# First stage of a gMLP, attention and MoE block on one core: x loaded first, and one half of the adaLN modulation summed on TensorE

## The chip, the cores and the metric

The kernel runs on one core of a Trainium2 chip. The metric is the device time of one execution in microseconds. It is written in Bass: each engine (TensorE, VectorE, ScalarE, GpSimd, and SyncE, which only issues transfers) has its own program, and semaphores order them.

## The reference

One layer on x (512 rows of 1024, f32), with a conditioning vector c. What matters here is its beginning:

```python
sc = silu(c)
mod = sc @ w_ada + b_ada                    # 1024 -> 6*1024
sh1, sc1, ga1, sh2, sc2, ga2 = split(mod, 6)
h = rmsnorm(x, g_pre_mix) * (1.0 + sc1) + sh1
proj = h @ w_in                             # 1024 -> 2560
...                                         # gMLP and attention branches, output projection
x = x + ga1 * rmsnorm(mixed @ w_out, g_post_mix)
h = rmsnorm(x, g_pre_ffn) * (1.0 + sc2) + sh2
...                                         # 64 experts, top 8, and a shared one
x = x + ga2 * rmsnorm(y, g_post_ffn)
```

## The kernel before

**Modulation.** w_ada is read in 24 pieces of 1 MB: six channels in the order SC1, SH1, GA1, SC2, SH2, GA2, four pieces each. A piece holds two of the eight k slices (128 partitions x 2 x 1024). VectorE weighs it (`weigh_piece`): for each slice, acc = slice * sc_col[k] + acc, in L1365 (the first slice) and L1367 (the others). acc then holds, for each partition, a partial sum; TensorE sums over the partitions. For the first two channels that is done in column form, eight matmuls of one moving column for each channel (L966), so that a1c and b1c (128x8) hold scale and shift by partition. For the four later channels `modulation_row` (L978) sums with a stationary tile of ones into rows.

**Loads.** SyncE issues c, pieces 0 and 1, the four tiles of x, and then the other pieces. Three slots hold the pieces (n modulo 3 up to n=8, then modulo 2), and a piece waits until VectorE has weighed the one that was in its slot (`ada_used`). w_in comes in ten pieces of 1 MB through GpSimd's queue into two buffers (L543); the first two wait until six pieces of w_ada have been weighed.

**h1.** ScalarE sums the squares of x (L691). VectorE, after its third piece, forms the rms factor (`factor`, L1342 to L1350), and ScalarE scales x into z1 (L697). TensorE waits for all four tiles of z1, transposes them in groups k=0 to 6 (`h1_transposes`, L949; seven PSUM banks, the eighth holds the columns), runs the column matmuls, and transposes group 7 into bank 4 once that has been read. VectorE makes a1c and b1c (L1395 to L1398, `ab_ok`). ScalarE then applies them for each k (L712), and VectorE splits the result into a high and a low part (L1409, L1410).

**w_in.** Each piece is split as well: ScalarE makes the high part (`piece_high`, L704), VectorE and GpSimd half of the low part each (`piece_low` L1403; L548). ScalarE and VectorE take up piece 0 behind k=3 of the h1 loop. `project(i)` (L1000) needs both low parts, and `project(0)` the first four k; it runs 48 matmuls. From the third piece on, VectorE alternates between `piece_low`, the norm of v and two pieces of w_ada for each piece of w_in.

Everything behind the projections (attention, output projection, router, 64 experts) is unchanged.

Of the kernel before, what the change touches and what calls it, by code (L numbers as in the profile page):

```python
# [21 lines left out]
F32 = mybir.dt.float32  # L22
# [3 lines left out]
ALU = mybir.AluOpType  # L26
# [9 lines left out]
WO_RING = 3  # L36
DG = 512
# [24 lines left out]
def block_kernel(nc, x, c, w_ada, b_ada, g_pre_mix, w_in, ln_sgu_g, ln_sgu_b, w_spatial, b_spatial,  # L62
                 g_branch, w_out, g_post_mix, g_pre_ffn, w_router, router_bias, w_gate, w_up,
                 w_down, ws_gate, ws_up, ws_down, g_post_ffn, out):
    with ExitStack() as ctx:
# [6 lines left out]
        def at(name, shape, dt, off):  # L72
# [11 lines left out]
        ada = [at("ada0", [P, 2, D], F32, 0), at("ada1", [P, 2, D], F32, 8 * KB),  # L84
               at("ada2", [P, 2, D], F32, 136 * KB)]
# [139 lines left out]
        vec_in = sem("vec_in")  # L225
        row_in = sem("row_in")
        grow_in = sem("grow_in")
        ada_in = [sem(f"ada_in{s}") for s in range(3)]
# [121 lines left out]
        def ada_slot(n):  # L350

            slots = [m % 3 if m < 9 else m % 2 for m in range(n + 1)]
            same = [m for m in range(n + 1) if slots[m] == slots[n]]
            return slots[n], len(same), same[-2] if len(same) > 1 else None

        CHUNKS = [SC1, SH1, GA1, SC2, SH2, GA2]
# [48 lines left out]
        def _(sp):  # L405
            sp.dma_start(c_col[:, :], c.rearrange("(p k) -> p k", k=KD)).then_inc(c_in, 16)
            for n in range(4 * len(CHUNKS)):
                g, q = CHUNKS[n // 4], n % 4
# [3 lines left out]
                slot, _, before = ada_slot(n)  # L412
# [8 lines left out]
                sp.dma_start(ada[slot][:, :, :], ada_v[:, 2 * q:2 * q + 2, g * D:(g + 1) * D])\  # L421
                  .then_inc(ada_in[slot], 16)

# [77 lines left out]
        def _(gp):  # L501
# [32 lines left out]
            for i in range(PIECES + 1):  # L534
                if i < PIECES:
                    if i == 0:
                        gp.wait_ge(ada_used, 6)
                    if i >= 2:
                        gp.wait_ge(wphi_ok, i - 1)
                        gp.wait_ge(wplo_dve, i - 1)  # L540
                        gp.wait_ge(wplo_pool, i - 1)
# [114 lines left out]
        def _(ac):  # L656
# [19 lines left out]
            with nc.allow_non_contiguous_dma(reason="two short vectors by column"):  # L676
                load(gb[:, :], g_branch.rearrange("(k p) -> p k", p=P))
                load(bsp[:, :], b_spatial.rearrange("g i -> i g"))
# [20 lines left out]
            def piece_high(i):  # L699

                ac.wait_ge(win_in[i % 2], 16 * (i // 2 + 1))
                if i >= 2:
                    ac.wait_ge(proj_mm, 4 * (i - 1))
                A(wphi[:, i % 2], wraw[:, i % 2], ACT.Copy).then_inc(wphi_ok, 1)  # L704


            ac.wait_ge(ab_ok, 1)
            for k in range(KD):
# [5 lines left out]
                if k == KH - 1:  # L714
                    piece_high(0)
# [26 lines left out]
            ac.wait_ge(ada_used, 9)  # L742
# [202 lines left out]
        def _(pe):  # L945
# [13 lines left out]
            for k in range(KD - 1):  # L959
                h1_transposes(k)  # L960

            for ch in range(2):
                pe.wait_ge(acc_ok, ch + 1)
                cols = acc[:, ch, :].rearrange("p (q k) -> p k q", k=KD)
                for k in range(KD):
                    ins = mm(ps[:, 7 * BANK + ch * KD + k:7 * BANK + ch * KD + k + 1], cols[:, k, :],  # L966
                             ones[:, 0:1], start=True, stop=True)
                ins.then_inc(mod_mm, 1)
# [3 lines left out]
            def modulation_row(ch):  # L972

                pe.wait_ge(acc_ok, ch + 1)
# [47 lines left out]
            pe.wait_ge(vec_in, 16 * 6)  # L1022
# [301 lines left out]
        def _(v):  # L1324
# [29 lines left out]
            def weigh_piece(n):  # L1354

                ch, q = n // 4, n % 4
                if q == 0 and ch >= 2:
                    v.wait_ge(mod_mm, ch - 1)
                slot, count, _ = ada_slot(n)
                v.wait_ge(ada_in[slot], 16 * count)  # L1360
                for r in range(2):
                    k = 2 * q + r
                    src = ada[slot][:, r, :]
                    if k == 0:
                        ins = V.tensor_scalar(acc[:, ch % 2, :], src, sc_col[:, 0:1], None, ALU.mult)  # L1365
                    else:
                        ins = V.scalar_tensor_tensor(out=acc[:, ch % 2, :], in0=src, scalar=sc_col[:, k:k + 1],  # L1367
                                                     in1=acc[:, ch % 2, :], op0=ALU.mult, op1=ALU.add)
                    if r == 0:
                        then(ins)  # L1370
                    else:
                        ins.then_inc(ada_used, 1)
                        v.wait_ge(ada_used, n + 1)
# [421 lines left out]
```

## Time and profile before

| | |
|---|---|
| median of 3 executions | 1143.39 us (1142.51 to 1143.91) |
| profiled execution | 1143.01 us |
| its span | 1141.3 us |
| TensorE busy in the span | 1044.1 us (91%) |
| VectorE / ScalarE / GpSimd busy | 720.5 / 570.9 / 592.6 us |
| start of `project(0)` | 53.98 us |

The times in rows are microseconds from the start of the span. The 1.7 us between the span and the profiled execution's own time lie outside of the trace. PE is TensorE's matmul part, PEld its weight loads, DVE VectorE, ACT ScalarE, POOL GpSimd, SP SyncE; a name that ends in q is that engine's sequencer, where transfers are issued. L966 is line 966 of the kernel before. A matmul on f32 operands is recorded as two matmul instructions, one on fp32r operands as one.

### The profile page before, as it was taken

Reading aid. Unit: us, or ns where it says so; the run is one execution under the profiler, and the core shown is the slowest. Engines: PE = TensorE matmul, PEld = TensorE weight load, DVE = VectorE, ACT = ScalarE, POOL = GpSimd, SP = SyncE. Lnnn points to the kernel's source line nnn. Section 1 sums busy time; section 2 is a strip of 40 time slices with the busy share of each in tenths; the row PEclk is TensorE's granted clock in tenths of the full one; section 3 lists DMA queues with packets and bytes.
Section 4 is the critical chain, followed back from the end, with each engine's and each line's share of the span. In section 5 each row is a group of like instructions: output and inputs, shape, how many; then the busy total and the mean of one; then the engine's idle time right before and its main releaser. Section 6 shows DMA issues by size and latency. Waiting matters only on the chain.

```text
span 1141.3 us, 15074 instructions
## 1 busy us (share of the span) xinstructions
PE 1044.1 (91%) x4500; PEld 726.2 (64%) x4500; DVE 720.5 (63%) x1282; ACT 570.9 (50%) x605; POOL 592.6 (52%) x356
## 2 busy tenths in 40 slices
PE   0699897979798899999999999999999999999965
PEld 0587675547663677666766677666776677666522
DVE  4649785652755665777666666567676666586247
ACT  4334125652341466655655566655665666555401
POOL 0223222540221576667767776776767777667300
PEclk9699998889998999999999999999999999999988
DMA  9656851202152489999999999999999888899296
GB/s 322 246 178 243 293 203 47 74 28 84 74 221 82 159 323 370 351 369 378 353 377 366 369 351 346 351 375 388 328 364 350 345 327 338 344 352 351 87 389 273
DMA packets 68904, 318.67 MB, mean 279 GB/s; under 512 B 18640, under 2 KB 19152, under 8 KB 41360
## 3 DMA queue, kind: packets, MB, share of 16 engines
q1 hardware_dynamic: 42096, 267.41, 61.3%
q0 software_dynamic: 23104, 47.50, 11.3%
q10 hardware_dynamic: 3680, 3.46, 0.9%
q8 instruction: 13, 0.21, 0.1%
q14 instruction: 11, 0.09, 0.0%
HBM read 317.25 MB, written 39.85 MB: 313 GB/s over the span
## 4 chain that ended last, share of the span: by engine, by line
PE 73%; DVE 9%; DMA 8%; issue 4%; ACT 3%; POOL 2%; SPq 1%; ACTq 0%; DVEq 0%; POOLq 0%
PE ps L1234 18%; PE ps L1215 10%; PE ps L1217 9%; PE ps L1216 9%; PE ps L949 7%; PE ps L1000 7%; DMA yall<-y_rows 4%; DMA rawd<-in_w_down_dram 3%; PE ps L1150 2%; PE ps L1125 2%; DVE acc L1367 1%; PE ps L1082 1%; PE ps L1056 1%; DMA ada<-in_w_ada_dram 1%; PE ps L1170 1%
## 5 line engine op out<-in xcount | busy, mean ns | idle before, releaser
L585 POOL DMA_INDIRECT hg<-h_rows,idxg x70 | 212.1, 3030 | 140.0 <-DVE idxg L1675 139.7
L827 ACT ACTIVATE whi<-raw 128x2048 fp32r<-128x2048 f32 x136 | 260.6, 1917 | 21.2 <-issue 10.4
L1681 DVE TENSOR_TENSOR wlo<-raw,whi 128x1536 fp32r<-128x1536 f32 x134 | 257.5, 1947 | 12.1 <-ACT whi L827 11.8
L1234 PE MATMUL ps<-rawd,actt 128*128 128x512 f32 x544 | 244.8, 592 | 2.0 <-ACT actt L863 1.4
L1215 PE MATMUL ps<-whi,hthi 128*128 128x512 f32 x544 | 225.2, 414 | 1.9 <-POOL wlo L600 1.9
L1695 DVE TENSOR_TENSOR htlo<-ps,hthi 128x1024 fp32r<-128x1024 f32 x68 | 83.2, 1224 | 206.3 <-ACT hthi L859 206.3
L1217 PE MATMUL ps<-whi,htlo 128*128 128x512 f32 x544 | 213.0, 392 | 0.0
L1216 PE MATMUL ps<-wlo,hthi 128*128 128x512 f32 x544 | 212.8, 391 | 0.0
L600 POOL TENSOR_TENSOR wlo<-raw,whi 128x512 fp32r<-128x512 f32 x134 | 208.0, 1575 | 1.9 <-ACT whi L827 0.2
L869 ACT ACTIVATE ysb<-ps 128x1024 f32<-128x1024 f32 x68 | 69.7, 1024 | 210.8 <-PE ps L1234 210.8
L1234 PEld LDWEIGHTS ps<-rawd,actt 128*128 128x128 f32 x544 | 102.5, 189 | 106.1 <-issue 97.8
L593 POOL DMA_INDIRECT y_rows<-ysb,idxs x68 | 72.8, 1070 | 100.0 <-ACT ysb L869 55.4
L1217 PEld LDWEIGHTS ps<-whi,htlo 128*128 128x128 f32 x544 | 102.1, 188 | 23.4
L1215 PEld LDWEIGHTS ps<-whi,hthi 128*128 128x128 f32 x544 | 102.2, 188 | 19.4 <-issue 2.0
L1216 PEld LDWEIGHTS ps<-wlo,hthi 128*128 128x128 f32 x544 | 102.7, 189 | 17.2
L949 PEld LDWEIGHTS ps<-ident,hg 128*128 128x128 f32 x552 | 64.6, 140 | 34.9 <-issue 34.8
L949 PE MATMUL ps<-ident,hg 128*128 128x128 f32 x552 | 71.6, 273 | 0.0
L859 ACT ACTIVATE hthi<-ps 128x1024 fp32r<-128x1024 f32 x68 | 69.5, 1022 | 0.7 <-PE ps L949 0.7
L1367 DVE SCALAR_TENSOR_TENSOR acc<-ada,sc_col,acc 128x1024 f32<-128x1024 f32 x42 | 62.9, 1499 | 8.7 <-DMA ada<-in_w_ada_dram 7.4
L548 POOL TENSOR_TENSOR wplo<-wraw,wphi 128x1024 fp32r<-128x1024 f32 x10 | 30.2, 3017 | 65.7 <-ACT wphi L704 65.6
L1660 DVE TENSOR_SCALAR s_onehot<-iotab,posb 128x128 bf16<-128x128 bf16 x284 | 52.6, 249 | 0.0
L560 POOL TENSOR_TENSOR wolo<-woraw,wohi 128x512 fp32r<-128x512 f32 x16 | 36.0, 2266 | 31.3 <-ACT wohi L797 24.9
(248 smaller groups left out, 1321.1 us busy)
## 6 DMA issues: line engine op xcount, KB each, us to landing
raw<-in_w_gate_dram SPq DMA_DIRECT2D x68, 1024.0 KB, 7.6
raw<-in_w_up_dram SPq DMA_DIRECT2D x68, 1024.0 KB, 10.5
rawd<-in_w_down_dram SPq DMA_DIRECT2D x68, 1024.0 KB, 12.8
ada<-in_w_ada_dram SPq DMA_DIRECT2D x24, 1024.0 KB, 6.9
yall<-y_rows SPq DMA_DIRECT2D x8, 2048.0 KB, 24.2
wraw<-in_w_in_dram POOLq DMA_DIRECT2D x10, 1024.0 KB, 5.8
woraw<-in_w_out_dram SPq DMA_DIRECT2D x16, 256.0 KB, 2.7
xs<-in_x_dram SPq DMA_DIRECT2D x4, 512.0 KB, 10.7
```

Source lines behind the costliest of these rows:

```text
L585: gp.indirect_dma_start(out=hg[s][:, :, :].rearrange("p k q -> p (k q)"), out_offset=None, in_=h_rows, in_offset=bass.IndirectOffsetOnAxis ...
L600: gp.tensor_tensor(wlo[s][:, :, c0:c1], raw[:, s, :, c0:c1], whi[:, s, :, c0:c1].bitcast(F32), ALU.subtract).then_inc(lo_pool, 1)
L827: A(whi[:, s, :, cols], raw[:, s, :, cols], ACT.Copy).then_inc(hi_ok, 1)
L949: return pe.transpose(o, i, ident[:, :])
L1000: ins = mm(bank(m), st, mv, start=(h == 0 and k == 0 and n == 0), stop=(h == 1 and k == KH - 1 and n == 2))
L1215: mm(out_, hthi[s][:, k, :], hi, start=(k == 0), stop=False)
L1216: mm(out_, hthi[s][:, k, :], lo, start=False, stop=False)
L1217: ins = mm(out_, htlo[s][:, k, :], hi, start=False, stop=(k == KD - 1))
L1234: ins = mm(bank(4 + hf), actt[:, k, :], rawd[:, s, k, hf * 512:(hf + 1) * 512], start=(k == 0), stop=(k == KF - 1))
L1367: ins = V.scalar_tensor_tensor(out=acc[:, ch % 2, :], in0=src, scalar=sc_col[:, k:k + 1], in1=acc[:, ch % 2, :], op0=ALU.mult, op1=ALU.add)
L1681: V.tensor_tensor(wlo[s][:, :, c0:c1], raw[:, s, :, c0:c1], whi[:, s, :, c0:c1].bitcast(F32), ALU.subtract).then_inc(lo_dve, 1)
L1695: V.tensor_tensor(htlo[s][:, :, :], bank(0, 2).rearrange("p (k q) -> p k q", k=KD), hthi[s][:, :, :].bitcast(F32), ALU.subtract).then_inc( ...
```

## The change

- SyncE issues c, all of x, and then pieces 0 to 5, without a wait, into six slots. Channels SH1 and SC1 alternate: even pieces n < 8 are shift, odd ones scale. Piece 6 goes into slot 0 and waits for `sh_mm` 1, piece 7 into slot 1 and waits for the first scale piece to be weighed. Behind piece 7 SyncE issues the first two pieces of w_in. The sixteen later pieces use two slots.
- The shift half is summed on TensorE: `shift_row(n)` multiplies with the stationary operand sc_col[:, k] (128x1) and 512 moving columns of the piece, four matmuls for each piece, into one row of banks 5 and 6. ScalarE copies the row to `sh_row` (1x1024), and eight matmuls with one contraction row bring it into column form.
- VectorE weighs only the scale pieces (four of the first eight), and forms the rms factor after the first of them.
- TensorE transposes five groups of z1 first, then the shift pieces, the shift columns and the scale columns, then groups 5 and 6.
- ScalarE makes the high part of w_in piece 0 between the row's copy and `ab_ok`, ahead of the h1 loop.
- The two short loads by column (gb, bsp) are issued by GpSimd, with a semaphore of their own.

```diff
-        ada = [at("ada0", [P, 2, D], F32, 0), at("ada1", [P, 2, D], F32, 8 * KB),
-               at("ada2", [P, 2, D], F32, 136 * KB)]
+        ada = [at(f"ada{s}", [P, 2, D], F32, (0, 8, 136, 112, 120, 128)[s] * KB) for s in range(ADA_SLOTS)]
+        sh_row = at("sh_row", [1, D], F32, 188 * KB)
...
+        FIRST = 8
+        ADA_SLOT = [0, 1, 2, 3, 4, 5, 0, 1] + [n % 2 for n in range(FIRST, 24)]
+        def ada_piece(n):
+            return (n % 2, n // 2) if n < FIRST else (n // 4, n % 4)
+        CHUNKS = [SH1, SC1, GA1, SC2, SH2, GA2]
...
 # SyncE
+            for t in range(TT):
+                sp.dma_start(xs[:, t, :], x[t * P:(t + 1) * P, :]).then_inc(x_in[t], 16)
             for n in range(4 * len(CHUNKS)):
-                if n == 2:
-                    for t in range(TT):
-                        sp.dma_start(xs[:, t, :], x[t * P:(t + 1) * P, :]).then_inc(x_in[t], 16)
-                if before is not None:
-                    sp.wait_ge(ada_used, before + 1)
+                g, q = ada_piece(n)
+                if n == FIRST:
+                    load_win(0)
+                    load_win(1)
+                if n == 6 or n == 8:
+                    sp.wait_ge(sh_mm, 1 if n == 6 else 4)
+                elif n == 7:
+                    sp.wait_ge(ada_used, 1)
+                elif n > 8:
+                    sp.wait_ge(ada_used, n - 5)
...
 # GpSimd
+                gp.dma_start(gb[:, :], g_branch.rearrange("(k p) -> p k", p=P)).then_inc(col_in, 16)
+                gp.dma_start(bsp[:, :], b_spatial.rearrange("g i -> i g")).then_inc(col_in, 16)
-            for i in range(PIECES + 1):
+            for i in range(1, PIECES + 1):
...
 # ScalarE
+            ac.wait_ge(sh_mm, 4)
+            A(sh_row[:, :], bank(5, 2)[0:1, :], ACT.Copy).then_inc(sh_ok, 1)
+            piece_high(0)
             ac.wait_ge(ab_ok, 1)
...
-                if k == KH - 1:
-                    piece_high(0)
...
 # TensorE
+            def shift_row(n):
+                _, q = ada_piece(n)
+                pe.wait_ge(ada_in[ADA_SLOT[n]], 16 * ada_count(n))
+                for r in range(2):
+                    k = 2 * q + r
+                    for hf in range(2):
+                        ins = mm(bank(5 + hf)[0:1, :], sc_col[:, k:k + 1], ada[ADA_SLOT[n]][:, r, hf * 512:(hf + 1) * 512],
+                                 start=(k == 0), stop=(k == KD - 1))
+                ins.then_inc(sh_mm, 1)
-            for k in range(KD - 1):
+            for k in range(5):
                 h1_transposes(k)
+            pe.wait_ge(sc_ok, 1)
+            for n in range(0, FIRST, 2):
+                shift_row(n)
+            pe.wait_ge(sh_ok, 1)
+            shifts = sh_row[:, :].rearrange("p (q k) -> p k q", k=KD)
+            for k in range(KD):
+                ins = mm(ps[:, 7 * BANK + KD + k:7 * BANK + KD + k + 1], shifts[:, k, :], ones[0:1, 0:1],
+                         start=True, stop=True)
+            ins.then_inc(mod_mm, 1)
+            pe.wait_ge(acc_ok, 1)
...
+            for k in range(5, KD - 1):
+                h1_transposes(k)
...
 # VectorE
-            for n in range(8):
+            for n in range(1, FIRST, 2):
                 weigh_piece(n)
-                if n == 2:
+                if n == 1:
                     factor(ST_X, D)
                     v.sem_inc(rs_x_ok, 1)
-            v.wait_ge(vec_in, 16 * 6)
+            v.wait_ge(vec_in, 16 * 4)
+            v.wait_ge(col_in, 16 * 2)
```

## Rows read from the trace of the kernel before

**Rows 1.** Busy time by stretch: start:end, length, busy (x instructions), clock, DMA.

```profile
350.00:1085.00 735.00, 727.16 (x3217) 502.48 (x3215) 470.88 (x931) 427.73 (x415) 495.30 (x278) 1.00 0.86 329
```

**Rows 2.** The chain of waits, first 120 us: start, length, what.

```profile
4.20 0.67 SPq L411
4.91 13.77 DMA ada<-in_w_ada_dram
18.77 1.29 DVE acc L1367
...
22.92 7.61 ACT z L697 x4
30.67 5.77 PE ps L949 x28
36.44 7.51 PE ps L966 x32
44.65 0.79 ACT h1f L712
...
53.98 24.75 PE ps L1000 x96
...
117.35 12.81 PE ps L1000 x48
```

**Rows 3.** DMA issues around 4.9, 25 and 4 us; last number: us to landing.

```profile
xs<-in_x_dram SPq DMA_DIRECT2D x1, 512.0 KB, 11.7
ada<-in_w_ada_dram SPq DMA_DIRECT2D x1, 1024.0 KB, 13.8
...
ada<-in_w_ada_dram SPq DMA_DIRECT2D x1, 1024.0 KB, 5.0
...
bsp<-in_b_spatial_dram ACTq DMA_DIRECT2D x1, 2.0 KB, 20.6
```

**Rows 4.** Timeline of VectorE and GpSimd, 10 to 60 us: start, length, instruction.

```profile
12.10 0.75 DVE L1365 TENSOR_SCALAR acc<-ada,sc_col 128x1024 f32<-128x1024 f32 x1 [12.10 <-ACT sc_col L680]
21.41 0.17 DVE L1342 TENSOR_SCALAR var<-stat 128x4 f32<-128x4 f32 x1
49.18 0.69 DVE L1410 TENSOR_TENSOR h1lo<-h1f,h1hi 128x512 fp32r<-128x512 f32 x1
50.45 1.23 DVE L1403 TENSOR_TENSOR wplo<-wraw,wphi 128x1024 fp32r<-128x1024 f32 x1 [0.58 <-ACT wphi L704]
50.50 3.37 POOL L548 TENSOR_TENSOR wplo<-wraw,wphi 128x1024 fp32r<-128x1024 f32 x1 [17.97 <-ACT wphi L704]
51.59 2.57 DVE L1409 CAST h1hi<-h1f 128x512 fp32r<-128x512 f32 x1
```

**Rows 5.** The chain of waits later on, 130 to 285 us.

```profile
130.16 1.72 PE ps L978 x4
...
158.89 0.87 PE ps L949 x8
...
197.84 4.56 PE ps L1056 x8
...
205.07 3.03 PE ps L1082 x8
...
238.75 0.98 PE ps L1090 x8
...
284.52 1.13 ACT o_sb L838
```

**Rows 6.** Stretches as in group 1; last three: granted clock, DMA share, GB/s.

```profile
30.00:40.00 10.00, 9.33 (x45) 9.37 (x45) 5.58 (x5) 0.52 (x1) 1.78 (x2) 0.96 1.01 378
...
59.00:60.00 1.00, 1.00 (x5) 0.76 (x4) 1.00 (x1) 0.00 (x0) 1.00 (x1) 0.63 0.31 115
...
118.00:119.00 1.00, 1.00 (x4) 0.78 (x3) 0.96 (x2) 0.00 (x0) 0.98 (x2) 0.50 0.07 29
...
206.00:208.00 2.00, 2.00 (x8) 0.83 (x6) 2.00 (x1) 1.50 (x3) 0.94 (x1) 0.87 0.00 0
```

More of the change, by code:

```diff
@@ L36 @@
 WO_RING = 3
+ADA_SLOTS = 6
 DG = 512
@@ L225, in block_kernel @@
         vec_in = sem("vec_in")
+        col_in = sem("col_in")
+        win_first = [sem(f"win_first{s}") for s in range(2)]
         row_in = sem("row_in")
         grow_in = sem("grow_in")
-        ada_in = [sem(f"ada_in{s}") for s in range(3)]
+        ada_in = [sem(f"ada_in{s}") for s in range(ADA_SLOTS)]
+        sh_mm = sem("sh_mm")
+        sh_ok = sem("sh_ok")
         ada_used = sem("ada_used")
@@ L349, in block_kernel, with ada_count @@
         SC1, SH1, GA1, SC2, SH2, GA2 = 1, 0, 2, 4, 3, 5
[L350 to L356, printed above, removed]
+        FIRST = 8
+        ADA_SLOT = [0, 1, 2, 3, 4, 5, 0, 1] + [n % 2 for n in range(FIRST, 24)]
+        def ada_piece(n):
+            return (n % 2, n // 2) if n < FIRST else (n // 4, n % 4)
+        def ada_count(n):
+            return ADA_SLOT[:n + 1].count(ADA_SLOT[n])
+        CHUNKS = [SH1, SC1, GA1, SC2, SH2, GA2]
         COLG = [DG, 0, 2 * DG, 2 * DG + 512, 2 * DG + 1024]
@@ L531, in _ @@
             gp.sem_inc(const_ok, 1)
-            for i in range(PIECES + 1):
[L535 to L541, printed above, removed]
+            with nc.allow_non_contiguous_dma(reason="two short vectors by column"):
+                gp.dma_start(gb[:, :], g_branch.rearrange("(k p) -> p k", p=P)).then_inc(col_in, 16)
+                gp.dma_start(bsp[:, :], b_spatial.rearrange("g i -> i g")).then_inc(col_in, 16)
+            for i in range(1, PIECES + 1):
+                if 2 <= i < PIECES:
+                    gp.wait_ge(wphi_ok, i - 1)
+                    gp.wait_ge(wplo_dve, i - 1)
+                    gp.wait_ge(wplo_pool, i - 1)
                     g, h = i // 2, i % 2
@@ L699, in piece_high @@
             def piece_high(i):
-                ac.wait_ge(win_in[i % 2], 16 * (i // 2 + 1))
+                if i < 2:
+                    ac.wait_ge(win_first[i], 16)
+                else:
+                    ac.wait_ge(win_in[i % 2], 16 * (i // 2))
                 if i >= 2:
@@ L1354, in weigh_piece @@
             def weigh_piece(n):
[L1356 to L1360, printed above, removed]
+                ch, q = ada_piece(n)
+                a = 0 if n < FIRST else ch % 2
+                if q == 0 and n >= FIRST:
+                    v.wait_ge(mod_mm, ch - 1 if ch > 2 else 2)
+                v.wait_ge(ada_in[ADA_SLOT[n]], 16 * ada_count(n))
                 for r in range(2):
                     k = 2 * q + r
-                    src = ada[slot][:, r, :]
+                    src = ada[ADA_SLOT[n]][:, r, :]
                     if k == 0:
-                        ins = V.tensor_scalar(acc[:, ch % 2, :], src, sc_col[:, 0:1], None, ALU.mult)
+                        ins = V.tensor_scalar(acc[:, a, :], src, sc_col[:, 0:1], None, ALU.mult)
                     else:
-                        ins = V.scalar_tensor_tensor(out=acc[:, ch % 2, :], in0=src, scalar=sc_col[:, k:k + 1],
-                                                     in1=acc[:, ch % 2, :], op0=ALU.mult, op1=ALU.add)
+                        ins = V.scalar_tensor_tensor(out=acc[:, a, :], in0=src, scalar=sc_col[:, k:k + 1],
+                                                     in1=acc[:, a, :], op0=ALU.mult, op1=ALU.add)
                     if r == 0:
```

32 lines of the change are left out of this document (14 added, 18 removed).

## The prediction

> **What bounds the kernel now.** I read the busy times by stage first [rows 1]: from 350 to 1085 us TensorE is busy 727 of 735 us, and nothing there is touched. The edit lies in front of the first projection. So the question is only when the first projection starts, and whether what follows moves with it.
>
> The chain of waits answers both [rows 2]. It runs from the third piece of w_ada, which lands at 18.7 us [rows 3], over VectorE (two products, then the rms factor), ScalarE's scaling of x (22.92 to 30.5), the 28 transposes (to 36.4), the two channels' column matmuls (to 43.95), a1c and b1c (44.6), half of the h1 loop, and `project(0)` at 53.98. Behind 53.98 every piece of the chain follows from the piece before it: TensorE to 78.7, ScalarE's evacuation and eight DMA issues, VectorE's weighing and layer norm, then TensorE again from 117.35. No wait there is for something that keeps its own time, so I let a shift of `project(0)` pass through at full size. The moved w_ada pieces need a check: with two slots piece n=10 is requested only when n=8 has been weighed, while before it had been in a slot since about 45 us. It is used a round of VectorE's loop later; a round goes with a projection piece, 24.75/2=12.4 us [rows 2], and a transfer with nothing ahead takes 5.0 [rows 3]. That is covered by 7 us.
>
> **The change, step by step (times of the profiled execution).**
> *x ahead, scale piece next.* Queue SP carried two pieces and x first; the last x landed at 4.20+11.7=15.9. The same 4 MB now go out as x, shift piece 0, scale piece 1, so piece 1 lands at 15.9. One MB more landed 2.8 us later (18.7) [rows 3]; pieces 2 to 5 land at 18.7, 21.5, 24.3, 27.1. ScalarE is free early (the long issue of bsp leaves its queue) and has its squares done by about 12; that is worth nothing, because VectorE's factor stands behind piece 1: 15.9+0.75+1.30=18.0, factor 1.5 (21.4 to 22.9 before), so z starts at 19.5 and ends at 27.1 (7.6 us for four) [rows 2, 4]. Here 3.4 us are won. The column loads on GpSimd's queue are needed at 50 us; the slower of the two took 20.6 us on the old queue [rows 3], and GpSimd has nothing else to do: zero.
>
> *What TensorE now does before piece 6 may be asked for.* SP's wait for n=6 is on `sh_mm`, the end of shift piece 0. TensorE comes to that only after `z_ok` and 20 transposes, 20x0.206=4.1 us: 31.2. Queue SP is then stuck with piece 7 and both w_in pieces behind it, and the DMA engines, busy all the time from 30 to 40 us before [rows 6], have nothing from 27.1 on.
>
> *Price of a shift piece.* It is 4 matmuls of 512 moving columns in f32. The nearest rows are the modulation rows: two such matmuls, recorded as four, took 1.72 us at the full clock, 0.43 a record [rows 5]. A piece is 8 records: 3.4 us at 2.4 GHz and 6.9 at 1.2. The stationary operand has one column where that row had 128; I take the same price, since a record's length in these rows goes with its moving columns (0.43 for 512, 0.12 for one). Bounds: above, the same; below, the one-column record, 0.12 (a piece 1.0 us, 1.9 at half).
>
> *Which clock.* The early rows run at 1.2 GHz though the granted clock reads 0.96 over 30 to 40: a transpose took 0.206 us then and 0.109 at 159 [rows 2, 5, 6]. The clock rose 5.6 us after `project(0)` began. In the attention stage it stayed low through 4.6 us of scores on 64 rows and rose about 1.2 us into the values' matmuls, whose stationary operand has 64 columns and 128 rows (they began at 205.07, the clock is up in 206 to 208) [rows 5, 6]. So a narrow stationary operand did not keep it low. I take a rise 3.5 us into piece 0 (bounds 1.2 and 5.6; never, as a rival). Half of 6.9 us is then done, the rest takes 1.7: piece 0 ends at 31.2+5.2=36.4.
>
> *Piece 6 onward.* Issued at 36.5, it lands after 5.0 us (a piece with nothing ahead of it [rows 3]): 41.5; piece 7 at 44.3, w_in 0 at 47.1, w_in 1 at 49.9. TensorE takes pieces 2, 4 and 6 without a gap: 36.4+3x3.44=46.7. ScalarE copies the row out of PSUM, 1.1 us as its 1024-column copy at 284 [rows 5]: 47.8. The eight shift columns are 16 records of 0.123 at the full clock, 2.0 us: 49.8. The scale half is ready (44.3+2.6=46.9), its columns take 2.0: 51.8. At 1.2 GHz these two would be 3.8 each (0.235 a record, as before).
>
> *A new collision.* ScalarE now makes wphi(0) ahead of the h1 loop: 47.8 to 49.7; GpSimd's wplo(0) runs 3.4 us, to 53.2. Before, a 512-column VectorE cast that came up while that instruction ran took 2.57 us and ended 0.3 after GpSimd (a subtraction of the same size, in another place, took 0.69); a1c's second operation, with two SBUF inputs, would meet it at 52.0. I count it held until 53.2: ab_ok at 53.6 instead of 52.4 [rows 4]. Nothing excludes a price of zero, so the low bound is 1.2 less.
> The Trainium skill (SBUF — State Buffer, "SBUF: two separate sides") says that VectorE and GpSimd share a port pair as an exclusive lock, which a VectorE operation with two SBUF inputs needs, and one with a PSUM input does not. By that rule a1c's first operation and b1c pass and only the second is held; the cast's row agrees that the loser waits to the end. With the rule the sum is as above, without it 1.2 us less.
>
> *The h1 loop.* Before, from ab_ok (44.6) four steps of VectorE went to 49.9, but wphi(0), placed at k=3, made wplo(0) end at 53.87, and that started `project(0)` [rows 4]. Now wplo(0) is done; only VectorE's own part of 1.23 stands behind the fourth step: 5.3+1.25, so `project(0)` starts 6.6 behind ab_ok where it was 9.4. 2.8 us are won. The two transpose groups behind the columns and the last group (bank 4) fit in these 6.6 us. wplo(1) still follows the h1 loop and so trails `project(0)` by what it did; the chain shows the two projections without a gap.
>
> *Sum.* 53.6+6.6=60.2, against 53.98: +6.2. In parts: z 3.4 us earlier; 8 transposes fewer ahead 1.6; shift rows 15.5; copy 1.1; columns 3.5 cheaper at the full clock; collision 1.2; h1 loop 2.8 cheaper: -3.4-1.6+15.5+1.1-3.5+1.2-2.8=+6.5, which agrees within the rounding of the handovers. The profiled execution took 1143.01 (span 1141.3), the median of the others is 1143.39, so I add to the median: 1149.6. I leave `project(0)`'s own slow 5.6 us as they are: the engine again has about 5 idle us ahead of it.
>
> **Rivals.**
> *The clock never rises on the shift rows* (1.2 GHz throughout). For it: one column of the array is far less than the 64 of the values' rows, and 5.8 us of transposes and 7.5 us of one-column matmuls did not raise it [rows 2]. Pieces 4x6.9=27.5: 31.2 to 58.7; copy 59.8; columns 7.6: 67.4; ab_ok 68.1; `project(0)` 74.7: +20.7, 1164.
> *The clock is still high when `project(0)` begins.* The old one lost 5.6/2=2.8 us there. For it: TensorE is now busy until 53 rather than 44. Against it: after the pause ahead of 117.35 the clock read 0.50 from 118 on, and here about 5 idle us lie ahead of `project(0)` [rows 2, 6]. +3.4: 1146.8.
> *Columns at 1.2 GHz.* The clock falls again while one-column matmuls run: 7.6 for 4.0, the collision gone: +8.7, 1152.1. This, and a piece 6 that lands 2.4 us later than I count (an estimate; 1.6 of it is hidden behind pieces 2 and 4), are the upper side of my own case.
> *Not slower: the one-column stationary operand is cheap.* At 0.235 us a record a piece is 1.9: piece 0 ends at 33.1, piece 6 lands at 38.1, piece 7 at 40.9, the row is out at 41.2, columns to 45.7 at the full clock, ab_ok 46.4 if nothing holds it, `project(0)` 53.0: -1.0, 1142.4. It decides only if a shift record costs under about 0.25 us and the collision is absent (GpSimd would run to 49.3). The moving rows of the modulation matmuls speak against it [rows 5].
> *The loss is swallowed later*, 1143.4: some wait behind 53.98 would need a clock of its own. The row loads and the w_ada pieces are the candidates, but all are requested by events that shift too, and the chain of before waits for none of them between 53.98 and 117.35.
>
> **How the numbers follow.** My case 0.64, with its upper side; clock still high 0.12; never rises 0.10; cheap operand 0.05; swallowed 0.04; something that I don't see 0.05. A measurement tells about 0.2% (2.3 us) from no change. My case, the high clock and the never-rising clock are all slower; with half of the unseen: 0.88. Cheap operand, swallowed: same 0.08 after giving a little to each side; faster 0.04. My own case's bounds: early rise and no collision take 2.3 off, to 1147.3; late rise (+1.1), slow piece 6 (+0.8) and slow columns (+2.5) add 4.4, to 1154.0. The range reaches down over the high clock with an early rise (1145.5) and up to 1156.5 for a rise later than the rows above show; the never-rising clock stays out.
>
> **What the profile of the changed kernel would show.** z from 19.5 to 27; SP's wait for n=6 ending on TensorE at about 36, with the DMA engines near empty from 27 to 38; shift records that come every 0.86 us and from within piece 0 on every 0.43; `project(0)` at about 60; first evacuation of v at about 85. Wrong if z starts near 13 (factor not held by piece 1), if piece 6 is issued before 31, if shift records stay at 0.86 or show 0.25, or if `project(0)` moves by 6 and the end does not.

## The result, and the profile after

| | before | after |
|---|---|---|
| median (6 runs each, taken side by side) | 1143.07 us (1141.3 to 1144.6) | 1148.37 us (1146.72 to 1149.18) |
| ratio, 95% interval | | 1.0047 [1.0029, 1.0065] |
| profiled span | 1141.3 us | 1147.5 us |
| start of `project(0)` | 53.98 us | 63.88 us |
| last vv row evacuated | 182.5 us | 190.7 us |
| last read of y_rows asked for | 1088.95 us | 1097.49 us |

The changed kernel is slower by 5.3 us in the median and by 6.2 us in the span. The forecast was 1149.6 us, and the sign, the time and the range hold. The way there holds less well: `project(0)` moved by 9.9 us where 6.2 were forecast, and 3.7 of those were given back before the end.

The chain of waits of the changed kernel, for the same stretch as [rows 2], with two rows of its end (start, length, what):

```profile
3.71 13.72 DMA ada<-in_w_ada_dram
17.53 0.76 DVE acc L1407
18.32 1.29 DVE acc L1409
21.15 7.49 ACT z L716 x4
28.77 4.50 PE ps L972 x20
33.27 14.51 PE ps L989 x32
47.80 1.02 ACT sh_row L730
48.87 3.96 PE ps L1001 x16
52.83 3.91 PE ps L1007 x16
57.47 0.79 ACT h1f L737
...
63.88 24.32 PE ps L1042 x96
...
1097.49 38.34 DMA yall<-y_rows
```

L989 is `shift_row`, L1001 the shift columns, L1007 the scale columns, L972 the transposes, L1042 `project`. The order is the one that the prediction drew: piece 1, factor, z, transposes, shift rows, copy, columns, h1 loop. VectorE has left it from 19.6 to 57 but for the factor and a1c; the 14.5 us of L989 stand where nothing stood before.

SyncE's waits in the changed kernel (engine and line, what it waited for: us, times, longest), and the stretches around the moved work, columns as in [rows 1]:

```profile
SPq L442 <- PE ps L989: 34.4, 2, 26.5
```

```profile
26.00:28.00 2.00, 0.00 (x0) 0.00 (x0) 0.32 (x1) 2.00 (x2) 0.00 (x0) 1.00 0.11 43
30.00:32.00 2.00, 2.00 (x12) 2.00 (x11) 0.29 (x1) 0.00 (x0) 0.00 (x0) 1.00 0.00 0
51.00:52.00 1.00, 1.00 (x6) 1.00 (x6) 0.00 (x0) 0.00 (x0) 1.00 (x1) 0.82 1.02 414
52.00:54.00 2.00, 2.00 (x10) 1.99 (x10) 0.00 (x0) 0.00 (x0) 1.04 (x1) 0.50 1.02 414
```

The moved matmuls and the columns of the changed kernel by line (duration ns min/median/max, first and last start, forms), the first row for 33.2 to 34.2 alone:

```profile
L989 PE MATMUL ps<-ada,sc_col x2: 881/946/1011, 33.2 to 34.0; 128*1 128x512 f32 x2
L989 PE MATMUL ps<-ada,sc_col x32: 592/592/1011, 33.2 to 47.2; 128*1 128x512 f32 x32
L1001 PEld LDWEIGHTS ps<-ones,sh_row x16: 307/330/331, 48.9 to 52.4; 1*128 1x128 f32 x16
L1001 PE MATMUL ps<-ones,sh_row x16: 371/371/392, 48.9 to 52.5; 1*128 1x1 f32 x16
L1007 PE MATMUL ps<-ones,acc x16: 376/376/397, 52.8 to 56.3; 128*128 128x1 f32 x16
```

The 32 records of L989 fill 14.51 us; from about 34.7 on they come every 0.43. The DMA engines, at 1.01 from 30 to 40 before [rows 6], carry nothing from about 27 to 38: queue SP stands at piece 6, which waits for the end of shift piece 0, and piece 7 and both w_in pieces stand behind it. That was forecast. It looks like the fault of this design; the experiments say that it is not.

### The profile page after: what moved, and what is told of

The parts are those of the page before. It is cut to its first block, busy times and chain, and to the rows that moved or that the text cites. A ratio compares the mean times of both kernels' runs of the same rounds, so it can differ in the third digit from the quotient of the medians.

```text
span 1147.5 us, 15128 instructions
## 1 busy us (share of the span) xinstructions
PE 1059.3 (92%) x4532; PEld 729.5 (64%) x4532; DVE 710.6 (62%) x1274; ACT 571.5 (50%) x606; POOL 588.2 (51%) x356
## 4 chain that ended last, share of the span: by engine, by line
PE 77%; DVE 9%; DMA 6%; issue 3%; ACT 2%; POOL 1%; SPq 1%; ACTq 0%; DVEq 0%; POOLq 0%
PE ps L1276 19%; PE ps L1257 11%; PE ps L1259 10%; PE ps L1258 10%; PE ps L972 7%; PE ps L1042 7%; DMA yall<-y_rows 3%; PE ps L1192 2%; PE ps L1167 2%; PE ps L1124 1%; DMA rawd<-in_w_down_dram 1%; DVE acc L1409 1%; PE ps L989 1%; PE ps L1098 1%; DMA ada<-in_w_ada_dram 1%
## 5 line engine op out<-in xcount | busy, mean ns | idle before, releaser
L607 POOL DMA_INDIRECT hg<-h_rows,idxg x70 | 186.2, 2660 | 141.7 <-DVE idxg L1718 139.4
L622 POOL TENSOR_TENSOR wlo<-raw,whi 128x512 fp32r<-128x512 f32 x134 | 230.3, 1741 | 2.1 <-ACT whi L850 0.3
L972 PEld LDWEIGHTS ps<-ident,hg 128*128 128x128 f32 x552 | 64.6, 141 | 35.0 <-issue 34.8
L972 PE MATMUL ps<-ident,hg 128*128 128x128 f32 x552 | 71.6, 273 | 0.0
L1409 DVE SCALAR_TENSOR_TENSOR acc<-ada,sc_col,acc 128x1024 f32<-128x1024 f32 x35 | 53.9, 1540 | 24.3 <-DMA ada<-in_w_ada_dram 23.4
## 6 DMA issues: line engine op xcount, KB each, us to landing
rawd<-in_w_down_dram SPq DMA_DIRECT2D x68, 1024.0 KB, 13.3
```

What stands on the lines that cost most here:

```text
L607: gp.indirect_dma_start(out=hg[s][:, :, :].rearrange("p k q -> p (k q)"), out_offset=None, in_=h_rows, in_offset=bass.IndirectOffsetOnAxis ...
L622: gp.tensor_tensor(wlo[s][:, :, c0:c1], raw[:, s, :, c0:c1], whi[:, s, :, c0:c1].bitcast(F32), ALU.subtract).then_inc(lo_pool, 1)
L972: return pe.transpose(o, i, ident[:, :])
```

## The experiments

All were timed in five rounds against the kernel before. The theory behind the prediction (T) says that the change loses because TensorE takes up the shift pieces only after z and the transposes, and needs longer for them than it took for what was removed. Its first rival says that the DMA pause sets the end.

**1. Eight slots, so that SyncE stops for nothing before piece 8.** From the changed kernel:

```diff
-(0, 8, 136, 112, 120, 128)[s] * KB) for s in range(ADA_SLOTS)]
+(0, 8, 136, 112, 120, 128, 176, 96)[s] * KB) for s in range(ADA_SLOTS)]
...
-                if n == 6 or n == 8:
-                    sp.wait_ge(sh_mm, 1 if n == 6 else 4)
-                elif n == 7:
+                if n == 8:
+                    sp.wait_ge(sh_mm, 1)
+                elif n == 9:
                     sp.wait_ge(ada_used, 1)
...
```

> Changed kernel, but eight slots: pieces 6 and 7 and both w_in pieces are issued without a wait. Theory 1 (the loss is TensorE's order: it takes up the four shift pieces one behind the other after the transposes, 33.3 to 47.8 us, and no piece is late for it): project(0) stays at 63.9, within 0.5, and the time is that of the changed kernel, 1148.4, though piece 7 is weighed at about 31 to 35 instead of 45.7 and the pause of the DMA engines from 26 to 38 us is gone. Theory 2 (the loss is SyncE's wait for n=6 and the pause behind it): project(0) comes 5 to 10 us earlier and the time falls to 1139 to 1144.

Measured: 1147.5 us, ratio 1.0035 [1.0022, 1.0047]; `project(0)` at 62.37. A stretch and the chain:

```profile
26.00:28.00 2.00, 0.00 (x0) 0.00 (x0) 0.55 (x1) 2.00 (x2) 0.00 (x0) 1.00 1.03 412
```

```profile
20.84 7.48 ACT z L716 x4
28.46 3.98 PE ps L972 x20
32.43 13.84 PE ps L989 x32
```

The pause is gone, DMA share 1.03 where it was 0.11, and VectorE took up its last scale piece at 32.6 instead of 45.75. The shift rows still start at 32.4 and `project(0)` is only 1.5 us earlier, where T had allowed 0.5 and the rival had asked for 5 to 10. The 1.5 us are no wait of SyncE's: z starts 0.3 earlier, the same 20 transposes take 3.98 us for 4.50, and the shift rows 13.84 for 14.51, as the matmuls reached the fast pace within the transposes and not within the rows. Such a difference comes without any edit too: the 28 transposes of the old kernel take 5.77 us in its own profile, 5.03 in that of experiment 8 and 4.63 in that of experiment 7. A difference of 1 us in `project(0)` between two profiles is therefore no evidence by itself. The pause was hidden behind TensorE's own queue: the rival falls.

**2. The shift pieces as they land.** From the changed kernel; TensorE takes pieces 0, 2 and 4 ahead of its wait for z, and piece 6 behind the transposes:

```diff
-            pe.wait_ge(z_ok, TT)
...
-            for k in range(5):
-                h1_transposes(k)
             pe.wait_ge(sc_ok, 1)
-            for n in range(0, FIRST, 2):
+            for n in range(0, FIRST - 2, 2):
                 shift_row(n)
+            pe.wait_ge(z_ok, TT)
+            for k in range(5):
+                h1_transposes(k)
+            shift_row(FIRST - 2)
```

> Changed kernel, but TensorE takes shift pieces 0, 2 and 4 as they land, ahead of its wait for z and the transposes; only piece 6 stays behind them. Theory 1 (order on TensorE): three pieces, 10 to 11 us, leave the path; transposes end at 33.3, piece 6 is done at 37 to 40, project(0) at 53 to 56, 8 to 10.5 us earlier than 63.9. The time is then 1138 to 1141 if the 4 us that the changed kernel showed less at the end than at project(0) belong to the change, 1142 to 1144 if they were chance of its last read and of ScalarE's issues. Theory 2 (the DMA pause): the same direction, as piece 6 is asked for at about 22, so only its agreement with the eight-slot run decides between the two.

Measured: 1135.05 us, 0.9927 [0.9910, 0.9945]. The chain:

```profile
5.45 19.50 DMA ada<-in_w_ada_dram
...
24.99 3.59 PE ps L988 x8
...
28.63 2.40 PE ps L972 x20
31.03 3.54 PE ps L988 x8
```

`project(0)` starts at 50.67, 13.2 us ahead of the changed kernel (8 to 10.5 were expected), and the time follows by 13.3. Two things add up: three pieces lie under the wait for z, and the matmuls have reached the fast pace before the transposes, 20 of which take 2.40 us (0.120 each) instead of 4.50. The same matmuls, slots, loads and columns, in another order, turn a loss of 5 us into a gain of 8. That is the largest effect of the study, and T's main point. Against the kernel before only 3.3 of the span's 8.4 us are won at `project(0)`; 2.2 more have come by the last vv row, and 2.3 by a faster last read (38.42 us for 40.70), on which see experiments 9 and 10.

**3. The factor ahead of the first scale piece.** From the changed kernel:

```diff
+            factor(ST_X, D)
+            v.sem_inc(rs_x_ok, 1)
             for n in range(1, FIRST, 2):
                 weigh_piece(n)
-                if n == 1:
-                    factor(ST_X, D)
-                    v.sem_inc(rs_x_ok, 1)
```

> Changed kernel, but VectorE forms the rms factor before piece 1, as soon as the squares of x are summed (12 us). z then runs from 13.5 to 21, the transposes to 25.5, the shift pieces 0, 2 and 4 follow as they have landed (the last at 25), and piece 6 is asked for at about 30. Theory 1 (order on TensorE, headed by z): project(0) 7 us earlier than 63.9, at 56 to 57.5, time 1140.5 to 1142. Rival: z is not what TensorE's chain hangs on (it waits for shift pieces or for piece 6 instead), project(0) at 60 or later, time 1145 and more.

Measured: 1141.05 us, 1.0001 [0.9989, 1.0013]; `project(0)` at 56.86. The chain:

```profile
14.59 7.45 ACT z L716 x4
22.17 4.50 PE ps L972 x20
26.67 14.09 PE ps L989 x32
```

z starts 6.6 us earlier, everything behind it moves by as much or a little more, and the loss is gone from the time. It is not gone from the first stage: `project(0)` is still 2.9 us later than in the kernel before, and the last read, 38.35 us for 40.70, gives most of that back. x had been there and squared since about 12; the factor, a chain of 0.17 us operations, stood behind 1 MB of w_ada.

**4. Both orders together.** Experiment 2 with the edit of experiment 3:

> Both: shift pieces 0, 2, 4 taken up as they land, and the factor before piece 1. With z ready at 21 TensorE's transposes come after piece 4 (landed at 25) instead of at 28.6, so piece 6, which lands at about 30, is the next bound. Theory: project(0) at 49.5 to 50.7, 0 to 1.2 us earlier than with the landing order alone, time 1134 to 1135. Rival: piece 6 lands as early as 28, then 2.4 us earlier, time 1132.5.

Measured: 1128.98 us, 0.9915 [0.9881, 0.9948], the lowest median of the kernels that compute the reference; its six executions spread from 1126.4 to 1137.8. The chain:

```profile
28.49 2.33 PE ps L972 x20
30.83 3.54 PE ps L988 x8
34.39 1.02 ACT sh_row L730
35.45 3.96 PE ps L1002 x16
39.41 3.91 PE ps L1008 x16
```

Here `project(0)` is at 50.47, 0.2 earlier than in experiment 2: there already the transposes followed piece 4's matmuls (24.99+3.59=28.58), so the earlier factor has nothing left to give. The time is 6 us lower all the same. The last vv row came at 173.1 (177.0 in experiment 2), and half of that difference is one place where VectorE weighs a piece; its timeline there, first of experiment 2 and then of this one:

```profile
82.08 9.40 DVE L1410 SCALAR_TENSOR_TENSOR acc<-ada,sc_col,acc 128x1024 f32<-128x1024 f32 x4
```

```profile
80.81 7.38 DVE L1410 SCALAR_TENSOR_TENSOR acc<-ada,sc_col,acc 128x1024 f32<-128x1024 f32 x4
```

The same four products take 9.40 and 7.38 us: two of them meet GpSimd's subtraction and last 3.3 us each in experiment 2, one does in this one, and the others take 1.3. The two kernels' intervals overlap, so a gain of this one over experiment 2 is not shown.

**5. Columns from a contiguous stationary operand.** A column matmul loads every eighth element of `acc` or `sh_row` as its stationary operand, since feature p*8+k belongs to column k. From the changed kernel, here it loads 128 neighbours:

```diff
-            shifts = sh_row[:, :].rearrange("p (q k) -> p k q", k=KD)
+            shifts = sh_row[:, :].rearrange("p (k q) -> p k q", k=KD)
-            cols = acc[:, 0, :].rearrange("p (q k) -> p k q", k=KD)
+            cols = acc[:, 0, :].rearrange("p (k q) -> p k q", k=KD)
```

> Changed kernel, but the 16 column matmuls read their stationary operand as 128 neighbouring elements instead of every eighth; the columns then hold the wrong features, so the output is not the reference's, and the time is read for the price alone. Theory A (the price of 0.247 us a record is that of a strided weight load, whatever the clock): 0.12 to 0.15 us a record at the full clock, the two groups take 4 to 5 us instead of 7.9, project(0) at 60 to 61, time 1145 or so. Theory B (the low clock): 0.24 us a record as before, project(0) at 63.9, time 1148.4.

The features get each other's scale and shift, which changes the routing (536 expert transposes instead of 552), so only the first stage is read; the time, 1125.72 us, can't be set beside the others. `project(0)` starts at 60.20, within the 60 to 61 of theory A. The rows of the two column lines, to set beside those of the changed kernel above:

```profile
L1001 PEld LDWEIGHTS ps<-ones,sh_row x16: 181/187/187, 48.0 to 49.7; 1*128 1x128 f32 x16
L1001 PE MATMUL ps<-ones,sh_row x16: 245/245/266, 48.0 to 49.7; 1*128 1x1 f32 x16
L1007 PEld LDWEIGHTS ps<-ones,acc x16: 186/333/333, 49.9 to 52.6; 128*128 128x128 f32 x16
```

The columns take 5.1 us instead of 7.9. In the changed kernel the granted clock read 1.00 until about 51.6, past the middle of the shift columns, and 0.50 under the scale columns, at nearly one price: 0.247 and 0.244 us a record (3.96/16, 3.91/16). With a contiguous operand a record costs 0.122 at the high clock and about 0.21 once the clock has fallen (at about 50.3 in this run). So the strided load sets the price, and these rows show no difference by the clock in it.

**6. Strided writes instead of strided loads.** Experiment 4, with both column groups read as 128 neighbours and the permutation moved into the copy of the row and into VectorE's last product:

```diff
-            A(sh_row[:, :], bank(5, 2)[0:1, :], ACT.Copy)
+            A(sh_row[:, :].rearrange("p (k q) -> p q k", k=KD), bank(5, 2)[0:1, :].rearrange("p (q k) -> p q k", k=KD), ACT.Copy)
+                    if n == FIRST - 1 and r == 1:
+                        ins = V.scalar_tensor_tensor(out=acc[:, 1, :].rearrange("p (k q) -> p q k", k=KD), ...
```

> The best kernel with the sum on TensorE (shift pieces on landing, factor first), and both column groups read 128 neighbouring elements: ScalarE's copy and VectorE's last product write their result in that order, so the output is the reference's. By the price measured (1.9 us for the first group, 3.1 for the second, in which the clock fell, against 7.9) project(0) comes 2.8 us earlier, at 47.7, time 1126 against 1129. Rival: the writes with a stride of 32 bytes cost on ScalarE and VectorE what the weight loads save: project(0) at 50.

Measured: 1132.08 us, 0.9907 [0.9883, 0.9931]; `project(0)` at 49.44. The chain:

```profile
34.88 1.91 ACT sh_row L730
36.83 1.94 PE ps L1002 x16
38.77 3.51 PE ps L1008 x16
```

The columns save 2.4 us (5.45 for 7.87), the second half of them at the pace of the low clock; the copy pays 0.9 us for the stride, and piece 4 landed 0.5 later. 1.0 us of the expected 2.8 remains at `project(0)`, nothing that can be told in the time.

**7. w_in piece 0 split ahead of the h1 loop, alone.** From the kernel before:

```diff
+            piece_high(0)
             ac.wait_ge(ab_ok, 1)
...
-                if k == KH - 1:
-                    piece_high(0)
```

> Kernel before, with one part of the change alone: ScalarE makes wphi(0) ahead of its wait for ab_ok, not behind k=3 of the h1 loop. My step: project(0) starts 6.4 to 6.6 us behind ab_ok instead of 9.4, so 2.8 earlier, at 51.2, if nothing collides. GpSimd's subtraction then runs from about 42 to 45.5, over a1c at 44.05: with the collision of the prediction a1c's second operation ends at about 45.5, and project(0) starts at 52.3. Time 1140.3 without and 1141.5 with it, against 1143.1. Rival: no gain, because wphi(0) waits for a w_in piece that lands only at 40 to 44 us and delays the loop.

Measured: 1137.6 us, 0.9959 [0.9936, 0.9982]; `project(0)` at 50.29. The handover from `ab_ok` (43.89) to `project(0)` takes 6.4 us, as in the changed kernel. GpSimd's half lies ahead of it:

```profile
41.28 2.35 POOL L548 TENSOR_TENSOR wplo<-wraw,wphi 128x1024 fp32r<-128x1024 f32 x1 [8.39 <-ACT wphi L704]
```

It ends within a1c (43.27 to 43.66), which isn't held. `project(0)` is 3.7 us earlier than in the kernel before. 3.0 of them are this handover (9.4 before), so this part of the change is worth its 3 us, as counted; the rest is the transposes' 4.63 us for 5.77, less the 0.4 by which z starts later.

**8. x ahead, alone.** From the kernel before:

```diff
+            for t in range(TT):
+                sp.dma_start(xs[:, t, :], x[t * P:(t + 1) * P, :]).then_inc(x_in[t], 16)
             for n in range(4 * len(CHUNKS)):
-                if n == 2:
-                    for t in range(TT): ...
```

> Kernel before, with x issued ahead of pieces 0 and 1, and nothing else. My step: worth nothing, because VectorE's factor stands behind its third piece, which still lands at 18.7: z from 22.9, project(0) at 54.0, time that of the kernel before. Rival: GpSimd's first w_in loads or VectorE's catching up gain 1 us or more. It also tells whether the load order is what makes the last read of y_rows land after 38.4 instead of 40.7 us, and ScalarE's seventh row load issue in 0.46 instead of 1.1 us, since neither of the two other parts did.

Measured: 1142.66 us, 1.0003 [0.9985, 1.0022]; z from 23.38, `project(0)` at 53.70. Nothing, since the factor stays behind the third piece.

**9. and 10. What made the end come back?** The last read of y_rows takes 38.3 us to land in the changed kernel and 40.7 in the one before, and two small loads on ScalarE's queue near 82 to 92 us are issued in 0.46 us each instead of 1.26 and 0.77. Two parts of the change could have done it: the column loads that went to GpSimd's queue, or the w_in pieces that went to SyncE's.

```diff
 # 9, GpSimd
+                gp.dma_start(gb[:, :], ...).then_inc(col_in, 16)
+                gp.dma_start(bsp[:, :], ...).then_inc(col_in, 16)
 # 10, SyncE
+                if n == 8:
+                    for i in range(2):
+                        sp.dma_start(wraw[:, i], ...).then_inc(win_first[i], 16)
```

> Kernel before, with the two short column loads (gb, bsp) issued by GpSimd, and nothing else. They are 1,536 of the 3,680 packets of ScalarE's DMA queue. In both profiles of the old load order ScalarE's seventh row load took 1.26 and 1.08 us to issue and its eighth 0.77 and 0.83; in four profiles of the changed order both took 0.46 to 0.55. Theory Q (the slow issue belongs to the number of packets that went through ScalarE's queue before): both take 0.46 to 0.55 here too, the stretch from project(0) to the last evacuation of the projections is 1 us shorter, and the last read of y_rows still lands 40.7 us behind its issue. Rival (it belongs to when w_in or w_ada pieces travel): the issue stays at 1.1 us and more. ScalarE is free 8 us earlier, which changes nothing, as VectorE's factor waits for the third piece. Time 1141.5 to 1142.8.

> Kernel before, with the first two pieces of w_in issued by SyncE behind w_ada piece 7, and nothing else: 1,056 packets more on SyncE's queue. In both profiles of the old kernel family the last 2 MB read of y_rows landed 40.7 and 41.0 us behind its issue, in four profiles of the changed one 38.3 to 38.4. Theory Q (the last read's duration goes with what the queue has carried before it): it lands at 38.4 here, and the stretch from the last experts to the end is 2.4 us shorter; time about 1140.5. Rival (something else of the change, the column loads or the slots, makes it shorter): 40.7 to 41.0, time 1143.

Measured: 1142.13 us, 1.0009 [0.9994, 1.0023], and 1141.67 us, 0.9999 [0.9978, 1.0021]. The last read lands after 40.9 and 40.5 us: neither is the cause. Nor is x ahead (experiment 8: 41.2). The changed kernel and the six experiments built on it show 38.3 to 38.4, the one before and the six built on it 40.5 to 41.2.

**11. The order alone, without TensorE's sum.** The kernel before with x first, the factor ahead of piece 0, `piece_high(0)` early and the column loads on GpSimd:

```diff
+            factor(ST_X, D)
+            v.sem_inc(rs_x_ok, 1)
             for n in range(8):
                 weigh_piece(n)
-                if n == 2: ...
```

> Kernel before with three slots and both halves still summed on VectorE, but in another order: x first, the two column loads on GpSimd, the factor before piece 0, wphi(0) ahead of the h1 loop. Theory 1 (what the first stage needs is order, not the sum on TensorE): z ends at 21, transposes at 27, VectorE ends piece 7 at 37 as the transfers allow, only the second channel's columns (3.8 us) follow, ab_ok at 41.5, project(0) at 48: 2.5 us ahead of the best kernel with the sum on TensorE (50.5). Time 1130 to 1134. Rival: VectorE falls behind the transfers when all eight pieces are its own and the factor comes first, ends piece 7 at 39 or later, project(0) at 50 or more.

Measured: 1139.64 us, 0.9984 [0.9968, 1.0001]; `project(0)` at 50.16. The last read lands after 41.1 us. A new wait has taken the place of the old; the chain, and the timeline of VectorE and GpSimd:

```profile
30.73 9.69 DMA wraw<-in_w_in_dram
```

```profile
42.43 2.34 POOL L552 TENSOR_TENSOR wplo<-wraw,wphi 128x1024 fp32r<-128x1024 f32 x1 [10.20 <-ACT wphi L705]
43.12 1.93 DVE L1409 CAST h1hi<-h1f 128x512 fp32r<-128x512 f32 x1 [1.32 <-ACT h1f L714]
```

w_in piece 0 is still asked for when six pieces have been weighed (30.7), lands at 40.4, and now holds ScalarE, which stands at `piece_high(0)` with the h1 loop behind it. a1c and b1c are ready at 41.8, h1f starts at 42.26. And a collision of the predicted kind happens here, on the first cast: 1.93 us where later ones take 0.42, ended 0.3 after GpSimd. `project(0)` was expected at 48 and comes 2.2 us later; 0.3 of that stood at a1c already, the wait for w_in is 0.5 and the collision 1.5. The rival expected (VectorE late, at 39) did not come: it ended at 37.0. Even so `project(0)` is as early as in experiments 2 and 4.

**12. Experiment 11 with contiguous column loads** (VectorE writes its last product of either channel with the stride, into a buffer of its own):

> The order-only kernel with its column groups read as neighbouring elements; VectorE's last product of each channel writes that order. The second channel's columns are 1.9 us at the high clock or 3.5 at the low one, instead of 3.8: project(0) 0.3 to 1.9 us earlier than without. Rival: VectorE's strided product is longer than 1.3 us by as much or more: no gain or a loss.

Measured: 1139.95 us, 0.9975 [0.9957, 0.9993]; `project(0)` at 49.74. The chain:

```profile
35.51 1.97 DVE accp L1366
37.58 3.59 PE ps L967 x16
```

The strided product costs 0.7 us more than a plain one, and the columns, at the pace of the low clock, save 0.4 (3.59 us for 3.96): a1c and b1c are ready at 41.9, no earlier than in experiment 11, as the rival said. `project(0)` is 0.4 us earlier because w_in piece 0 landed that much earlier (40.0). Neither kernel with the old division of work comes near the time of experiment 4 (11 us apart in the medians and 8 by the ratios; they were not timed side by side), but that isn't won in this stage: `project(0)` starts within 0.7 us in all three. Of the 6.9 us between the spans of experiments 11 and 4, 4.4 have come by the last vv row and 2.8 by the last read. So what the sum on TensorE is worth by itself, once both orders are right, is not settled by these runs; it takes VectorE's work away, and its end (37.0 in experiment 11) no longer decides.

## Why the prediction was right, and where it wasn't

**The steps that held.** Piece 1 lands at 17.4 (forecast 15.9; no run shows why it took the 1.5 us more), and z runs 21.15 to 28.64 (19.5 to 27.1). SyncE's wait for n=6 ends on TensorE, and piece 6 is asked for at 37.5 (36.5) and is there in time. The price of a shift record, 0.43 us at the high clock whatever the width of the stationary operand, was right, and with it the rival "cheap operand" falls: the first records come about 0.86 us apart, those from 34.7 on 0.43. The pace doubled about 1.3 us into the work, near the early bound of 1.2 and not 3.5 as taken, so four pieces took 14.5 and not 15.5; "never rises" falls. (By [rows 6] that bound itself should have been 1.4: a clock of 0.87 over 206 to 208 puts the rise at 206.5.) "Still high at `project(0)`" falls too: 24.32 us for 24.75, and not 3.4 less. `ab_ok` to `project(0)` took 6.4 (6.6).

One reading of the prediction was wrong: that 5.8 us of transposes did not raise the clock in the kernel before. The last of its first 28 transposes (duration ns min/median/max) are short:

```profile
L949 PE MATMUL ps<-ident,z x12: 272/417/417, 34.1 to 36.2; 128*128 128x128 f32 x12
```

From 35.8 on they take 0.272 us instead of 0.417, so the pace had doubled before the columns began, and [rows 2]'s 0.206 is an average over both paces. The columns that followed show more: their weight loads, and two stretches of 1 us (last three numbers: granted clock, DMA share, GB/s):

```profile
L966 PEld LDWEIGHTS ps<-ones,acc x32: 312/335/336, 36.2 to 43.5; 128*128 128x128 f32 x32
38.00:39.00 1.00, 1.00 (x5) 1.00 (x6) 0.00 (x0) 0.00 (x0) 0.00 (x0) 1.00 1.04 418
42.00:43.00 1.00, 1.00 (x6) 1.00 (x5) 0.00 (x0) 0.00 (x0) 0.00 (x0) 0.50 1.00 397
```

The granted clock fell from 1.00 to 0.50 at about 39.3, in their midst, and each load took 0.335 us before and after. So the profile of before already held the evidence that the price of these columns does not go with the clock. Read rightly, the transposes would also have left "never rises" less than its 0.10.

**The sum at `project(0)`, term by term,** as measured: z 1.8 earlier, transposes 1.3 less, shift rows +14.5, copy +1.0, columns +0.4, collision 0, h1 loop 2.9 less: +9.9, as seen. Against the forecast's +6.5 the terms are off by +1.6, +0.3, -1.0, -0.1, +3.9, -1.2 and -0.1, together +3.4 (the forecast's other sum, 60.2, is off by 3.7).

**The mis-sized term** is "columns 3.5 cheaper at the full clock". I read the old columns' 0.235 a record as the price of the low clock and took 0.123 from L1090. But L1090 loads contiguous columns and these load every eighth element; at 1.00 and at 0.50 they cost 0.247 and 0.244 (experiment 5). The rival "columns at 1.2 GHz" had nearly the right time, 7.6 for 7.87, and the clock did fall at 51.6 as it said, but the fall was not what made the columns slow. The form of a row has to match in its access pattern, not only in its shape.

**The collision** did not happen in the changed kernel. GpSimd's subtraction (its row stands below) ended at 53.0, and a1c came only at 56.9 because of the slow columns. It also took 2.34 us, not the 3.37 of [rows 4], which held the time of VectorE's half beside it. That VectorE can be held in this way is seen in experiment 11. The Trainium skill (SBUF — State Buffer, "SBUF: two separate sides") states an exclusive lock of the port pair, for VectorE operations with two SBUF inputs and also for those in a mode that uses both ports. I weighed the first half alone. The cast that was held has one SBUF input, and passes 512 columns in 0.42 us (experiment 11) where the subtraction needs 0.69 [rows 4], which would fit the second half; that it ran in such a mode no run here shows.

**"I let a shift pass through at full size" failed.** Of +9.9 at `project(0)`, +8.2 is left at 125.51 against 117.35 [rows 2], +8.2 at the last vv row, +8.5 when the last read of y_rows is asked for, and +6.2 at the end of the span. Three parts have a place. The first two projections take 24.32 instead of 24.75 us: 0.4. ScalarE's small loads, in the timeline of the changed kernel, with GpSimd's subtraction of which I spoke above:

```profile
50.70 2.34 POOL L570 TENSOR_TENSOR wplo<-wraw,wphi 128x1024 fp32r<-128x1024 f32 x1 [44.38 <-ACT wphi L726]
...
91.12 0.46 ACTq L692 DMA_DIRECT2D rb<-in_router_bias_dram  x1
91.61 0.46 ACTq L773 DMA_DIRECT2D grow<-in_g_post_mix_dram  x1
```

The two loads took 1.26 and 0.77 before, and `piece_high` stands behind them: from the end of the second projection to wphi it is 92.52-88.20=4.3 us, where it was 84.29-78.73=5.6: 1.2 less before rounding. And the last read of y_rows took 38.34 us, in the kernel before 40.70 (its chain):

```profile
1088.95 40.70 DMA yall<-y_rows
```

That is 2.4 us. With 0.3 lost again on the way, 9.9-0.4-1.2+0.3-2.4 is the 6.2 of the span. (The 0.3 is no effect that can be told: from the last vv row to the asking for the last read the profiles with the reference's routing need 904.5 to 906.8 us, that of experiment 7 even 900.4.) So +6.2 was forecast and the span shows +6.2, although `project(0)` moved 3.7 us further than forecast; 3.7 us were given back behind it. That the two cancel was luck. The prediction's own sign of being wrong was `project(0)` moving by 6 without the end; what came was the reverse, the end moving by 6 and `project(0)` by 10. The rival "swallowed later" held for 3.7 of the 9.9 us. Why the small loads and the last read are shorter in every kernel built on the changed one stays open: four single parts of the change and two unions of them were put into the old kernel (experiments 7 to 12) and none brought it; the six slots and the sum of the shift half on TensorE were not tried there.

**What the loss is, shown.** It is not TensorE's sum in itself (experiments 2 and 4 keep it and are faster than the kernel before, by ratios of 0.9927 and 0.9915, 8 and 13 us in the medians), nor the DMA pause (experiment 1), but two orders: the shift rows behind z and the transposes (13 us), and the factor behind a scale piece (7 us where the rows stand behind z; they are not additive, since in experiment 4 piece 4's landing is the later event). The early split of w_in piece 0 is worth 3 us of the chain, x ahead alone nothing.

## What to carry to other kernels

When work moves to another engine, look first at what is queued ahead of it there: here the same matmuls stood on the path with 14.5 us behind a wait and with 7.1 when three of four pieces were taken as they landed, and the early work also had the matmuls at the fast pace for what followed. Loads brought forward are worth nothing while the operation that uses them stands behind a later one in its own program. Price a matmul from a row with the same access pattern of its stationary operand, and don't count on a shift of the front reaching the end in full size.

## What the runs showed of the hardware that was not expected

- A weight load of f32 with its elements 32 bytes apart is recorded at 0.330 us, at granted clock 1.00 and 0.50 alike; contiguous it is 0.187 at 1.00 and 0.333 at 0.50 (experiment 5). The strided ones are 0.330 with one contraction row and 0.334 with 128.
- At the start of a kernel the granted clock reads 1.00 while the records run at the pace of 1.2 GHz: the first two shift records of the changed kernel take 0.88 and 1.01 us in a stretch that reads 1.00, later ones come every 0.43.
- With its stationary operand one column wide, a record of 512 columns still takes 0.43 us in the changed kernel, as with 128 columns [rows 5], and the pace doubled 1.3 us into such records, with 4.5 us of transposes directly ahead of them.
- A write whose successive elements lie 512 bytes apart costs ScalarE 0.9 us more for 1024 elements of one partition (1.02 to 1.91, experiment 6), VectorE 0.7 more for 1024 on 128 partitions (1.29 to 1.97, experiment 12).
- GpSimd's subtraction takes 2.34 us when VectorE is not on its own half at the same time (changed kernel), and 3.37 when it is [rows 4].
